# Two head strips and a third conv strip in fp32, spare landing places for five blocks, and some work in another order

## The reference

```python
x = x + rms_norm(retention(rms_norm(x)))           # 4 heads: q, k of 256, v and gate of 512; w_in, w_out
x = x + (p[0] @ ple_w_proj[0]) * sigmoid(x @ ple_w_gate[0])
x = x + rms_norm(mla(rms_norm(x)))                 # 16 heads, latent attention; the gated heads @ mla_w_out
x = x + (p[1] @ ple_w_proj[1]) * sigmoid(x @ ple_w_gate[1])
mod = silu(c) @ w_ada + b_ada                      # six rows of 1024 that scale and shift
h = ln(x) * (1 + mod1) + mod0
a = causal_dwconv31(h[:, value] * sigmoid(h[:, gate]))  # "conv": value and gate are w_in strips
x = ln1(ALPHA * x + g1 * ((gate_a * a_branch + gate_b * pool_branch) @ w_out))
f = conv3(ln(x)*(1+mod4)+mod3 @ w_up); f = gelu(f2) * f1
x = ln2(ALPHA * x + g2 * (f @ w_down))
```

## Time and profile before

| | |
|---|---|
| median of 3 runs | 893.98 us (891.68 to 896.0) |
| the profiled execution | 889.62 us, its span from first to last instruction 887.8 us |
| mean granted clock of PE | 0.993 of 2.4 GHz |
| busy: PE / DVE / ACT / POOL | 859.1 / 665.5 / 494.8 / 50.5 us |
| DMA | 169.57 MB, mean 191 GB/s |

### The profile page before, as it was taken

One profiled execution on the slowest core, in us unless ns is written; L12 is line 12 of the kernel. 1 busy time (PEld: TensorE's weight loads), 2 busy tenths in 40 slices (PEclk: granted clock), 3 DMA queues, 4 the chain that ended last, 5 costly groups with the idle time before them and its releaser, 6 DMA issues.

```text
span 887.8 us, 15826 instructions
## 1 busy us (share of the span) xinstructions
PE 859.1 (97%) x5672; PEld 782.3 (88%) x5672; DVE 665.5 (75%) x928; ACT 494.8 (56%) x732; POOL 50.5 (6%) x61
## 2 busy tenths in 40 slices
PE   8999999999989999999999998999999899999995
PEld 7998999988868999999988788999988899999884
DVE  7869777676856777786866766799888588888565
ACT  6454544554646566657555545454743588888440
POOL 0018000000012000000000000070000000000000
PEclk8999999999999999999999999999999999999998
DMA  8756575668645747373658644534462565556551
GB/s 293 254 178 237 192 237 194 209 257 311 191 154 165 240 153 249 111 271 117 210 178 296 198 158 145 188 120 142 143 211 74 171 209 187 175 181 236 189 168 47
DMA packets 48432, 169.57 MB, mean 191 GB/s; under 512 B 5508, under 2 KB 6148, under 8 KB 48391
## 3 DMA queue, kind: packets, MB, share of 16 engines
q1 hardware_dynamic: 40612, 142.70, 48.2%
q10 hardware_dynamic: 7778, 26.32, 8.4%
HBM read 167.95 MB, written 1.05 MB: 190 GB/s over the span
## 4 chain that ended last, share of the span: by engine, by line
PE 80%; DVE 11%; DMA 3%; ACT 3%; issue 2%; POOL 0%; ACTq 0%; DVEq 0%; SPq 0%
PE bank L414 14%; PE bank L415 14%; PE bank L416 14%; PE bank L460 7%; PE bank L461 6%; PE bank L462 6%; DVE wlo L1366 3%; PE bank L427 2%; PE bank L804 2%; PE bank L716 1%; DMA ada_raw<-ada_in 1%; PE bank L609 1%; PE bank L610 1%; PE bank L611 1%; PE bank L719 1%
## 5 line engine op out<-in xcount | busy, mean ns | idle before, releaser
L877 ACT ACTIVATE whi<-raw 128x1024 fp32r<-128x1024 f32 (+1 forms) x259 | 268.1, 1041 | 247.0 <-PE bank L416 111.1
L1366 DVE TENSOR_TENSOR wlo<-raw,whi 128x1024 fp32r<-128x1024 f32 (+1 forms) x259 | 311.7, 1212 | 109.7 <-ACT whi L877 107.5
L414 PE MATMUL bank<-H,whi 128*128 128x256 f32 x928 | 269.4, 290 | 6.5 <-ACT WK L1324 3.0
L415 PE MATMUL bank<-H,whi 128*128 128x256 f32 x928 | 263.1, 284 | 0.0
L416 PE MATMUL bank<-H,wlo 128*128 128x256 f32 x928 | 263.1, 284 | 0.0
L414 PEld LDWEIGHTS bank<-H,whi 128*128 128x128 f32 x928 | 178.5, 192 | 7.9 <-DVE wlo L1366 5.4
L415 PEld LDWEIGHTS bank<-H,whi 128*128 128x128 f32 x928 | 178.6, 192 | 0.8 <-issue 0.2
L416 PEld LDWEIGHTS bank<-H,wlo 128*128 128x128 f32 x928 | 178.5, 192 | 0.0
L460 PE MATMUL bank<-whi,Y 128*128 128x512 f32 x216 | 84.3, 390 | 1.6 <-DVE Z L1721 1.6
L461 PE MATMUL bank<-wlo,Y 128*128 128x512 f32 x216 | 84.1, 389 | 0.0
L462 PE MATMUL bank<-whi,Y 128*128 128x512 f32 x216 | 84.1, 389 | 0.0
(11 more groups left out here) (255 smaller groups left out, 1276.6 us busy)
## 6 DMA issues: line engine op xcount, KB each, us to landing
raw<-w_head SPq DMA_DIRECT2D x48, 512.0 KB, 4.3
ada_raw<-ada_in ACTq DMA_DIRECT2D x48, 512.0 KB, 4.7
raw<-w_up SPq DMA_DIRECT2D x44, 512.0 KB, 3.3
raw<-w_down SPq DMA_DIRECT2D x22, 512.0 KB, 4.2
raw<-w_uq SPq DMA_DIRECT2D x24, 384.0 KB, 3.1
raw<-w_ret_out SPq DMA_DIRECT2D x16, 512.0 KB, 5.0
raw<-w_ple_gate SPq DMA_DIRECT2D x16, 512.0 KB, 4.4
raw<-w_mla_gate SPq DMA_DIRECT2D x16, 512.0 KB, 4.3
```

Of the source, the lines that this page charges most:

```text
L414: mm(o, whi[:, s, c], a[:, 0, :], start=start, stop=False)
L415: mm(o, whi[:, s, c], a[:, 1, :], start=False, stop=False)
L877: activation(whi[:, s, 0:n], raw[:, s, 0:n], ACT.Copy).then_inc(hi_done, 1)
L1366: tt(wlo[:, s, 0:n], raw[:, s, 0:n], f32(whi[:, s, 0:n]), ALU.subtract).then_inc(lo_done, 1)
```

## The change

1. The first two head blocks are plain strips. ACT and DVE copy the transposed tiles from PSUM into `WT` (`plain_quad`, `tensor_copy`), and `H`'s halves are made from there. The first head is taken out of PE's loop (`head_strips`, `head_rest`; the diff of their bodies is only the shift of the counts by `n0`). `hold` before the row is 4 instead of 8. ACT issues the five DMAs of constants after its splits of blocks 2 and 3 instead of before the high halves, and `p_hi(0)`, `p_lo(0)` come after the heads. ACT waits for block 4's low half before the heads.
2. Five blocks (`SPARE`) are loaded into `ada_raw` while no modulation block is in it: the fifth head block, two of the conv and two of the FFN; ACT and DVE split them from there.
3. The MLA out product makes the upper half of the columns first (`flip`, the weight's columns are rolled on the host), and waits for `mo_gated` only before the other half. `token_pass`, `both_tokens` and `square_half` take `h ^ flip` for `h`.
4. `sum_row(24)` stands between the transposes of the second `U_PRE1` tile and its products, no longer behind the QKV passes.
5. In both PLE gates DVE makes the first tile's low half ahead of `split(bj)`.
6. A third conv strip is plain; `B_WA + 1`'s first pass stands before the second tile's transposes; splits and value gates are written out in another order (on DVE `gated_value(n)` stands where ACT has `value_gate(n)`).
7. In LN1 DVE multiplies tile 1's last half by its row ahead of tile 0's `centred_rows`.
8. In the first FFN pass `conv_start(0)` stands ahead of `split(B_UP + 2)`.

```diff
 B_END = B_DN + FF_TILES
+SPARE = {B_HEAD + 4: 0, B_WA + 4: 0, B_WA + 5: 1, B_UP + 4: 0, B_UP + 5: 1}
+def raw_count(b):
+    return 16 * (b // RING + 1 - sum(x % RING == b % RING and x <= b for x in SPARE))
+def spare_count(b):
+    return 16 * sum(SPARE[x] == SPARE[b] and x <= b for x in SPARE)
...
+def block_in(b, n):
+    return ada_raw[:, SPARE[b], 0:n] if b in SPARE else raw[:, b % RING, 0:n]
...
+    def load_spare(b, src):
+        sp.dma_start(ada_raw[:, SPARE[b], :], src).then_inc(spare_loaded[SPARE[b]], 16)
...
     sp.dma_start(posi, pos_in.partition_broadcast(P)).then_inc(in_pos, 16)
-    load_some(B_HEAD, "head", 2, 12)
+    load_some(B_HEAD, "head", 2, 4)
+    load_spare(B_HEAD + 4, w["head"][4])
+    load_plain(B_HEAD, "head", 5, 6)
+    load_some(B_HEAD, "head", 6, 12)
...
     load_some(B_WA, "conv_in", 0, 4)
-    load_plain(B_WA, "conv_in", 4, 6)
-    load_some(B_WA, "conv_in", 6, 8)
+    sp.wait_ge(ada_used, 2 + 48)
+    load_spare(B_WA + 4, w["conv_in"][4])
+    load_spare(B_WA + 5, w["conv_in"][5])
+    load_plain(B_WA, "conv_in", 6, 7)
+    load_some(B_WA, "conv_in", 7, 8)
...
     load_some(B_UP, "up", 0, 4)
-    load_plain(B_UP, "up", 4, 8)
+    sp.wait_ge(lo_done, RING + B_WA + 6)
+    load_spare(B_UP + 4, w["up"][4])
+    load_spare(B_UP + 5, w["up"][5])
+    load_plain(B_UP, "up", 6, 8)
...
-    def out_product(base, y0):
-        both_tokens(base, 0, Y, 8, 8, [(y_ready, y0 + j // 2 + 1) if j % 2 == 0 else None for j in range(8)])
-        both_tokens(base, 1, Y, 8, 4)
-        token_pass(base, 0, 1, Y, 4, 8)
-        token_pass(base, 1, 1, Y, 4, 8)
+    def out_product(base, y0, flip=0, free=None):
+        both_tokens(base, 0, Y, 8, 8, [(y_ready, y0 + j // 2 + 1) if j % 2 == 0 else None for j in range(8)], flip)
+        if free is not None:
+            pe.wait_ge(*free)
+        both_tokens(base, 1, Y, 8, 4, (), flip)
+        token_pass(base, 0, 1, Y, 4, 8, (), flip)
+        token_pass(base, 1, 1, Y, 4, 8, (), flip)
...
     pe.wait_ge(const_ready, 1)
-    hold(PB[1], 8)
+    hold(PB[1], 4)
...
     turn_tile(U_PRE0, 1, WT, PB[3])
-    with pe.Fori(0, RET_HEADS) as i:
+    first = halves(free_d(V_HEAD))
+    plain_strip(B_HEAD, first[0], 0, [(plain_a, 1)] + [None] * 3 + [(plain_d, 1)])
+    plain_strip(B_HEAD + 1, first[1], 0)
+    plain_strip(B_HEAD, first[0], 1, [(plain_a, 2)] + [None] * 3 + [(plain_d, 2)])
+    plain_strip(B_HEAD + 1, first[1], 1)
+    b = free_d(V_HEAD + 1)
+    strip(B_HEAD + 2, halves(b)[0], H, before=h_waits(U_PRE0))
+    strip(B_HEAD + 3, halves(b)[1], H)
+    def head_strips(n0, i):
...
+    head_rest(0, 0)
+    with pe.Fori(0, RET_HEADS - 1) as i:
+        head_strips(1, i)
+        head_rest(1, i)
...
     turn_tile(U_PRE1, 1, WT, PB[1])
+    sum_row(24, PB[0])
...
     token_pass(B_MIN, 1, 1, H, 0, 4)
-    sum_row(24, PB[0])
...
     group(3, 0, 2)
-    pe.wait_ge(mo_gated, 4 * 4 + 1)
-    out_product(B_MO, RET_HEADS)
+    out_product(B_MO, RET_HEADS, 1, (mo_gated, 4 * 4 + 1))
...
     plain_strip(B_WA, first[0], 0, [(shifted_a, 1)] + [None] * 3 + [(shifted_a, 2)])
+    plain_strip(B_WA + 1, first[1], 0)
     turn_tile(U_LNA, 1, WT, PB[3])
-    plain_strip(B_WA + 1, first[1], 0)
+    third = halves(free_d(V_WA + 1))[0]
+    plain_strip(B_WA + 2, third, 0)
...
     plain_strip(B_WA + 1, first[1], 1)
-    for j in range(2, 8):
+    plain_strip(B_WA + 2, third, 1)
+    for j in range(3, 8):
...
             b = free_d(V_WA + j // 2)
-        strip(B_WA + j, halves(b)[j % 2], H, before=h_waits(U_LNA) if j == 2 else ())
+        else:
+            b = GD[j // 2 % 2]
+        strip(B_WA + j, halves(b)[j % 2], H, before=h_waits(U_LNA) if j == 3 else ())
...
         s = b % RING
-        act.wait_ge(raw_loaded[s], 16 * (b // RING) + 16 + 16 * (per // RING) * i)
+        if b in SPARE:
+            act.wait_ge(spare_loaded[SPARE[b]], spare_count(b))
+        else:
+            act.wait_ge(raw_loaded[s], raw_count(b) + 16 * (per // RING) * i)
         act.wait_ge(pe_done, b + 1 + per * i)
-        activation(whi[:, s, 0:n], raw[:, s, 0:n], ACT.Copy).then_inc(hi_done, 1)
+        activation(whi[:, s, 0:n], block_in(b, n), ACT.Copy).then_inc(hi_done, 1)
...
-            c = slice(512 * h, 512 * h + 512)
+            c0 = 512 * (h ^ flip)
+            c = slice(c0, c0 + 512)
...
             split(bg + 6)
+            split(bg + 7)
         else:
-            skip_split(2)
-        split(bg + 7)
+            skip_split(3)
...
         row_root_of(t, ssq[:, t, 0:1], D, eps[:, 0:1])
+    def plain_quad(t, b):
+        act.wait_ge(turned_psum, 2 * t + 1)
+        activation(WT[:, t, 0:512], b[:, 0:512], ACT.Copy).then_inc(plain_a, 1)
+    plain_quad(0, PB[2])
+    plain_quad(1, PB[3])
+    for t in range(2):
+        part_hi(t, 0, plain_a, t + 1)
+        part_hi(t, 1, plain_d, t + 1)
+    skip_split(2)
+    split(-1)
+    split(B_HEAD)
...
     act.dma_start(praw[:], p_in[0]).then_inc(in_p, 16)
-    for q in range(2):
-        hi_quad(U_PRE0, 0, q, PB[2])
-    split(-3)
-    for q in range(2):
-        hi_quad(U_PRE0, 1, q, PB[3])
-    split(-2)
-    split(-1)
-    split(B_HEAD)
-    p_hi(0)
...
+    act.wait_ge(lo_done, RING + B_HEAD + 5)
...
     activation(TAB[:, 2:4, :], mt, ACT.Sin).then_inc(trig_ready, 1)
+    p_hi(0)
...
+    out_rows(B_MO, K_MO, 40, 2, 1)
...
     activation(ROW_G2, PB[2][:], ACT.Copy).then_inc(g_ready, 1)
-    with act.Fori(0, 2) as i:
-        def value_gate(f, i):
-            act.wait_ge(dve_free, V_WA + 2 + 2 * i)
-            used(B_WA + 2 * f + 1, 4, i)
-            activation(SGT[:, f, 0:T], GD[f][:, T:2 * T], ACT.Sigmoid).then_inc(sgt_ready, 1)
-        for j in range(4):
-            split(B_WA + j, 1024, 4, i)
-            if j == 2:
-                value_gate(0, i)
-        value_gate(1, i)
+    def value_gate(n):
+        act.wait_ge(dve_free, V_WA + 2 + n // 2 * 2)
+        used(B_WA + 2 * n + 1)
+        activation(SGT[:, n % 2, 0:T], GD[n % 2][:, T:2 * T], ACT.Sigmoid).then_inc(sgt_ready, 1)
+    split(B_WA)
+    value_gate(0)
+    split(B_WA + 1)
+    split(B_WA + 2)
+    value_gate(1)
+    split(B_WA + 3)
+    split(B_WA + 4)
+    split(B_WA + 5)
+    value_gate(2)
+    split(B_WA + 6)
+    split(B_WA + 7)
+    value_gate(3)
...
     skip_split(4)
+    split(B_UP + 1)
     act.wait_ge(pads, 2)
-    split(B_UP + 1)
...
             gelu(i + o)
-        split(B_UP + 4 * o + 2, 1024, 4, i)
-        if o:
+            split(B_UP + 4 * o + 2, 1024, 4, i)
...
         conv_start(0)
+        if not o:
+            split(B_UP + 2)
...
         dve.wait_ge(hi_done, b + 1 + per * i)
-        tt(wlo[:, s, 0:n], raw[:, s, 0:n], f32(whi[:, s, 0:n]), ALU.subtract).then_inc(lo_done, 1)
+        tt(wlo[:, s, 0:n], block_in(b, n), f32(whi[:, s, 0:n]), ALU.subtract).then_inc(lo_done, 1)
...
-    def residual_half(t, h, row):
+    def gated_half(t, h, row):
...
         step(tt(WT[:, t, c], PB[2 + t][:, c], row[:, c], ALU.mult))
+    def residual_half(t, h, row):
+        gated_half(t, h, row)
+        added_half(t, h)
+    def added_half(t, h):
+        c = slice(512 * h, 512 * h + 512)
...
+        lo_tile(u, 0, PB[2])
         split(bj)
-        lo_tile(u, 0, PB[2])
...
         pre_rows(t, PB[0][:])
-    lo_tile(U_PRE0, 0, PB[2])
-    split(-3)
-    lo_tile(U_PRE0, 1, PB[3])
-    split(-2)
+    for t in range(2):
+        dve.wait_ge(turned_psum, 2 * t + 2)
+        nc.vector.tensor_copy(WT[:, t, 512:1024], PB[2 + t][:, 512:1024]).then_inc(plain_d, 1)
+    shifted_lo(U_PRE0, 0)
+    shifted_lo(U_PRE0, 1)
+    skip_split(2)
...
     ts(rt, rt, PI_IN, -PI_IN, ALU.min, ALU.max).then_inc(trig_arg, 1)
-    p_lo(0)
...
     mod_read(0, 0, 2, GD[1])
+    p_lo(0)
...
     variance(1)
-    skip_split(2)
-    split(B_PG1 + 7)
+    skip_split(3)
...
     first_norm(7, 0)
+    used(B_WO + 7)
+    gated_half(1, 1, ROW_G1)
     centred_rows(8, 0, True)
-    used(B_WO + 7)
-    residual_half(1, 1, ROW_G1)
+    added_half(1, 1)
...
 "uv": cat([_rows(uv[:, 512 * g:512 * g + 512]) for g in range(4)]), "uq": cat(uqs),
-"mla_out": _wide(mla_w_out[0]), "proj1": _wide(ple_w_proj[1]), "ple_gate1": _wide(ple_w_gate[1]),
+"mla_out": _wide(np.roll(mla_w_out[0], 512, axis=1)), "proj1": _wide(ple_w_proj[1]), "ple_gate1": _wide(ple_w_gate[1]),
```

More of the change, by code:

```diff
@@ L210, in program @@
         ada_loaded = [sem(f"ada_loaded{s}") for s in range(2)]
+        plain_a, plain_d = sem("plain_a"), sem("plain_d")
+        spare_loaded = [sem(f"spare_loaded{s}") for s in range(2)]
         ada_used, mod_psum, mod_done = sem("ada_used"), sem("mod_psum"), sem("mod_done")
@@ L467, in half, with token_pass @@
                 return PB[n + t][:, 512 * h:512 * h + 512]
-            def token_pass(base, t, h, a, j0, n, before=()):
+            def token_pass(base, t, h, a, j0, n, before=(), flip=0):
                 for j in range(j0, n):
@@ L476, in token_pass @@
                         pe.wait_ge(*before[j])
-                    last = row_products(b, half(2, t, h), t, a, 2 * j, j == 0, j == n - 1)
```

(49 more changed lines are left out.)

11 lines of the change are left out of this document (5 added, 6 removed).

## The result

| | before | after |
|---|---|---|
| median of 6 runs | 891.75 us (889.08 to 896.0) | 880.32 us (878.89 to 881.45) |
| profiled execution, its span | 889.62, 887.8 | 880.89, 879.1 |

The ratio is 0.9865, 95% interval 0.9848 to 0.9882: 1.35% faster, 12.0 us (10.5 to 13.6); between the two medians lie 11.4. The prediction was 885.2 (881.8 to 890.3): direction right, gain too small. The 4.9 between 885.2 and 880.32 have two parts. 2.2 are the base: I counted from 893.98, a median of three runs, and the median of six is 891.75. The rest is the gain. Between the two profiled executions it is 8.7, and the predicted sum was 8.8, so the question is where the other 3 us come from.

A forecast was written before the change was run, and what follows sets the result against it. PE was taken as the bound, busy 859.1 of 887.8 us, so gains were shorter waits or less matmul work. Terms a to h summed to 8.8, taken off the median 893.98 for 885.2, range 881.8 to 890.3.

The forecast's parts named there:

- b: First PLE gate: low half made ahead of the split, so PE's wait for H goes; gain 0.7 us.
- f: Conv strips: waits for the second LN tile and a gated value go, less a third plain strip's cost; gain 2.4 us.
- e: Second PLE gate: low half made ahead of the split, so PE's wait for H goes; gain 0.8 us.
- h: First FFN pass: the 3.0 wait for `conv_start(0)` goes, block 7 is late next; gain 1.1 us, bounds 0 and 2.8.
- g: LN1: `gated_half` ahead of `centred_rows` makes PE start later; a loss of 0.4 us, bounds -0.4 and 0.
- Rival 4: Whole kernel: with half the holds PE may start without the full clock; slower, 895.4 to about 899 us; chance 0.03.
- a: The start, first head: two plain strips let PE begin earlier; gain 1.4 us, bounds 0.5 and 2.7.
- theory B: Start, from a follow-up's forecast: half-clock stretches vary by run and the new start removes them; 4 to 5 us faster.
- c: QKV: `sum_row(24)` moved into the 1.0 wait for the second tile; gain 1.1 us, bounds 0.8 and 1.1.
- d: MLA out product: upper output half first, so the 1.6 wait for `mo_gated` goes; gain 1.7 us.
- Rival 2: Loads land in 3.3 and the angle chain frees the start; gain 11.5, so 882.5 us; chance 0.13.

## Why the prediction was off

**Right, by its own steps.** Every wait named as going is gone, and what was said to be late next is late: 0.3 twice for `wlo` near 28 and 31, one H wait of 1.1 in 250:265, 1.2 on the bank behind block 7; plain strips at 11.7, full clock behind them. Only LN1's wait was to be 1.7 to 1.8 and is 1.5. The terms b to f are within 0.2 of the landmarks, and b to e together, and f, within the intervals of the runs made for them.

**The step that failed** is the translation of the sum: "I take the difference off the median". It failed in its difference and in its median. The difference was worked out from one execution, 4.4 below that median, and I noted the gap without asking what it was made of. A part of it was the wait priced in term h: 3.0 idle in the profile, but in five of seven traces that have it the idle time and a stretch at 1.2 GHz. Term h, +1.1, is 1.9 in the landmarks and 4.2 (2.8 to 5.6) measured alone: this is the term that was mis-sized most, by a clock cost that it left out. Another part of the gap was the sample: three runs gave 893.98, the six of the result 891.75, all 82 timed executions of before 892.3. The sum of 8.8 taken off 891.75 is 883.0, still 2.6 too slow; that the base was 2.2 too high as well was bad luck, and without it the stated range would have reached down to 879.6. Of what h won beyond 1.1, 0.8 is that block 7 landed in 4.3 (issued 693.35, landed 697.68) where I had 4.4 to 5.9 and had charged g's delay; the clock adds 1.3 on the mean of the seven traces. Rival 4 had the clock as a danger only: it cost a fall made by the change, not one taken away by it. Its condition did come true for a while, for with half the holds PE had the full clock only from 11.06 on, where before had it from 5.40 (last section), but the spread row started 1.7 earlier and ended at the same time.

**Missed: mix block 7.** I took it that nothing between conv and LN1 moves. The wait for this block is 0.5 in the first profile of before but 0.5 to 1.8, mean 1.0, over nine traces of before and of kernels with some of the parts, and 1.9 and 1.4 in the changed kernel and in it without g. So the loss of 1.5 in the landmarks is some 0.7 between typical executions. Its cause, the rows ahead of it on SP's queue, is shown; why it grows when the stages before it run earlier is not.

**Mis-sized: a and g.** The first head's group sums come at 51.6 on the mean of nine traces with the old start and at 49.5 of eight with the new: 2.1, not 1.4. In three of the nine the spread row ran at half its pace (below) and the sums came at 52.6, in the other six at 50.9 to 51.3, and with the new start at 48.9 to 50.2. So part a wins 1.6 against most executions and 3.1 against some: theory B had a true core, too small for its 4 to 5. g costs 0.2 and not 0.4.

**The account**, where a, mix and the clock are from several executions and the rest from the two profiles: a 2.1, b 0.9, c 1.0, d 1.8, e 0.7, f 2.5, mix -0.7, g -0.2, h 1.9 and 1.3 of clock: 11.3, with 12.0 (10.5 to 13.6) measured. The mean of all traces without a part less the mean of those with it, stage by stage, gives 10.9. What remains is smaller than what the runs can tell. Rival 2's 882.5 was near, but by another way: its loads in 3.3 and its free start did not come.

## What to carry to other kernels

Take two or three profiled executions before costing a wait, and look at the granted clock behind each long wait of PE: such a wait (3 us here) is worth its idle time and often half as much again in matmuls at the lower clock, even where the one trace at hand doesn't show it. When a profiled execution is faster than nearly all runs, say what it lacks before taking differences from it, and don't hang a forecast on a median of three runs that span 4 us. A load that stands behind other loads on its queue is cheap to move, and its delay can be paid again by what is queued behind its split. A cost of 0.2 us can't be read from medians here, but from the distance between two landmarks in many traces it can.

## What the runs showed of the hardware

The spread row, four 512-column fp32 matmul instructions (0.43 each before in the first profile), in the timelines of before and after:
```profile
5.04 2.14 PE L586 MATMUL bank<-G,ones 1*128 1x512 f32 x4
```
```profile
3.34 3.78 PE L620 MATMUL bank<-G,ones 1*128 1x512 f32 x4
```
After, they start 0.86 apart (the first two 1.01), twice the distance, yet the clock of the window 3 to 8 us is given as 1.00 in both:
```profile
3.00:8.00 5.00, 5.00 (x10) 2.23 (x10) 1.17 (x3) 3.07 (x7) 0.00 (x0) 1.00 0.96 365
```
The packed traces hold the reason: their record of the clock doesn't begin with the kernel. In before it begins at 5.40 us, in after at 11.06, both times with the full clock, and a window without a record is printed as 1.00. In all 17 traces the row goes by this record: where it begins at 4.4 to 5.4 (six with the old start) the row runs 0.43 apart, where it begins at 10.4 to 13.6 (the other 11) it runs 0.86 apart. So at the start of a trace look at the distance between starts, not at the printed clock.

The half pace cost nothing in the changed kernel: the matmul behind the row starts at 7.04, and at 7.11 before. In the three traces with the old start and the row at half pace it starts near 8.75, and there the first head's sums come 1.5 late. Before has two stretches at the half clock in its start, 8.81 to 12.22 and 15.64 to 19.05, of which the prediction priced the second; the new start has none in eight traces.
